# Router logits with stationary weights, one piece behind the normalization, and an earlier load of the router weights

## The reference, cut to what matters

```python
x = x + g1 * mix_lat
h = rms_norm(x, norm2_g) * (1 + sc2) + sh2        # (2048, 1024) on a core
logits = (h @ router_w).astype(float32)           # router_w: (1024, 8)
top_val, top_idx = lax.top_k(logits, 2)
top_w = softmax(top_val)
out = sum over e of comb[:, e] * swiglu(h, w1[e], w3[e], w2[e])
```

## Time and profile before

| | us |
|---|---|
| median of the 3 runs shown | 4913.67 |
| lowest, highest of them | 4563.16, 5036.57 |
| profiled execution, its time | 4566.67 |
| its span on the slowest core (core 7) | 4565.6 |
| spans of the 8 cores | 4525.7 to 4565.6 |
| TensorE busy | 3878.8 (85%) |
| DVE busy, ACT busy, GpSimd busy | 1505.7, 1522.5, 523.0 |

### The profile page before, as it was taken

The page is one execution under the profiler, slowest core; times in us unless marked ns, Lnnn a source line. Parts: engine busy times, 40 slices in busy tenths (PEclk is TensorE's granted clock), DMA queues, the critical chain, the costliest instruction groups (busy, mean ns, idle before and its releaser), DMA issues.

```text
span 4565.6 us, 77498 instructions; the slowest of 8 cores (4525.7 to 4565.6 us)
## 1 busy us (share of the span) xinstructions
PE 3878.8 (85%) x28584; PEld 2519.2 (55%) x28584; DVE 1505.7 (33%) x2750; ACT 1522.5 (33%) x2399; POOL 523.0 (11%) x634
## 2 busy tenths in 40 slices
PE   4788889657999979888695376999999999999994
PEld 2345545433444434554344255777777778787773
DVE  3634452673223264334127232111111111111114
ACT  4678822554010277884126231111111111111110
POOL 0210000540000012000007212000000000000003
PEclk8999999868999999998896567999999999999997
DMA  9586653648884526999947507999999999999997
GB/s 240 86 111 107 107 93 65 93 65 120 120 113 81 97 44 91 110 109 109 118 65 98 74 1 264 312 310 318 308 320 306 320 307 321 304 320 310 312 309 248
DMA packets 112689, 822.84 MB, mean 180 GB/s; under 512 B 14496, under 2 KB 14768, under 8 KB 41408
## 3 DMA queue, kind: packets, MB, share of 16 engines
q0 software_dynamic: 31392, 280.83, 40.2%
q1 hardware_dynamic: 80928, 537.05, 35.0%
HBM read 1016.79 MB, written 217.06 MB: 270 GB/s over the span
## 4 chain that ended last, share of the span: by engine, by line
PE 73%; ACT 7%; issue 6%; DVE 6%; DMA 4%; POOL 2%; another core or an unknown queue 2%; DVEq 0%; ACTq 0%; POOLq 0%; SPq 0%
PE psall L273 65%; PE psall L270 5%; ACT attr L298 4%; PE psall L277 2%; DMA adaw<-ada_w 2%; DMA xstage<-x 1%; DVE ntmp L301 1%; DVE attr L334 1%; ACT hT L298 1%; DVE attr L301 1%; POOL wslot L301 1%; DMA attr<-ada_w 1%; POOL sigt L301 1%; ACT wslot L298 1%
## 5 line engine op out<-in xcount | busy, mean ns | idle before, releaser
L273 PE MATMUL psall<-hs,mslot 128*128 128x256 bf16 x10304 | 1130.6, 273 | 0.5 <-ACT hs L332 0.5
L273 PEld LDWEIGHTS psall<-hs,mslot 128*128 128x128 bf16 x10304 | 1009.2, 98 | 123.0 <-issue 0.7
L298 ACT ACTIVATE sig<-psall 128x512 bf16<-128x512 f32 x322 | 192.2, 597 | 1444.7 <-PE psall L273 1444.7
L298 ACT ACTIVATE attr<-psall 128x1024 bf16<-128x1024 f32 (+1 forms) x660 | 592.1, 979 | 183.0 <-PE psall L273 180.4
L273 PE MATMUL psall<-mslot,ysp 128*128 128x512 bf16 x2576 | 559.7, 379 | 0.0
L301 DVE TENSOR_TENSOR ysp<-sig,psall 128x512 bf16<-128x512 bf16 x322 | 221.3, 687 | 866.4 <-PE psall L273 844.0
L270 PE MATMUL psall<-vaug,attr 128*128 128x129 bf16 x4640 | 393.1, 228 | 61.8 <-issue 29.3
L273 PEld LDWEIGHTS psall<-mslot,ysp 128*128 128x128 bf16 x2576 | 251.2, 98 | 298.5
L270 PEld LDWEIGHTS psall<-vaug,attr 128*128 128x128 bf16 x4640 | 278.0, 100 | 209.0 <-issue 207.4
L273 PE MATMUL psall<-hT,fslot 128*128 128x512 bf16 (+1 forms) x1760 | 352.0, 363 | 0.9 <-ACT ftf L298 0.9
L273 PE MATMUL psall<-hT,wslot 128*128 128x512 bf16 (+1 forms) x1248 | 282.6, 373 | 41.4 <-DMA wslot<-w_in 36.0
(11 more groups left out here) (190 smaller groups left out, 3611.3 us busy)
## 6 DMA issues: line engine op xcount, KB each, us to landing
mslot<-mwb SPq DMA_DIRECT2D x483, 1024.0 KB, 6.8
mwb<-mw POOLq DMA_DIRECT2D x168, 1024.0 KB, 14.9
adaw<-ada_w POOLq DMA_DIRECT2D x32, 512.0 KB, 14.9
wslot<-w_in POOLq DMA_DIRECT2D x14, 1024.0 KB, 15.6
fslot<-f POOLq DMA_DIRECT2D x7, 2048.0 KB, 17.2
xslots<-cf SPq DMA_DIRECT2D x1, 11776.0 KB, 40.6
xst<-xslots POOLq DMA_DIRECT2D x23, 512.0 KB, 11.9
oslots<-otok POOLq DMA_DIRECT2D x23, 512.0 KB, 8.3
```

The costliest lines, as they stand in the source:

```text
L273: self.P.add("pe", lambda e: e.matmul(out.ap, lhsT.ap, rhs.ap, start=start, stop=stop), reads=[lhsT, rhs], writes=[out])
L298: self.P.add("act", lambda e: e.activation(out.ap, in_.ap, func, **kw), reads=rd, writes=wr)
```

## The change

The router weights and `iota` are loaded by the SP queue instead of GpSimd's, at the start of the second layer's scan, behind a fence at which SP waits for the other engines; their place in SBUF is moved to one that is free from there on. The product is turned round: the weights, 128 x 8, are stationary and 512 normalized rows stream, one `mm` for a chunk instead of four, with the logits as [8, 512]. It is issued one piece later, so that chunk c - 1 is multiplied behind the normalization of chunk c, and `nhf` has three buffers. After chunk 7 DVE copies [8, 512] from PSUM to `lgT`, and after the last tile 16 f32 transposes of 8 x 128 bring the logits back to rows of tokens.

```diff
-    P.fence(("act", "dve", "pool"))
+    P.fence(("act", "dve", "pool", "sp") if last else ("act", "dve", "pool"))
+    if last:
+        self.wr = self.at("wr", [128, 8, 8], F32, OW + 15360)
+        self.iota_t = self.at("iota", [128, 32], F32, OW + 15616)
+        iota_d = self.din("iota", [128, 32])
+        self.dma("sp", self.iota_t.v(0), DV(iota_d[:, :], [Buf("d")]))
+        self.dma("sp", self.wr.v(0), DV(self.router_d[l // 2, :, :].rearrange("(k p) e -> p k e", p=128), [Buf("d")]))
...
-    wr = self.at("wr", [128, 8, 8], F32, OW + 8192)
-    iota_t = self.at("iota", [128, 32], F32, OW + 8448)
-    nhf = self.at("nhf", [128, 2, 512], F32, OR + 11264)
-    self.dma("pool", iota_t.v(0), DV(iota_d[:, :], [Buf("d")]))
-    self.dma("pool", wr.v(0), DV(router_d[l // 2, :, :].rearrange("(k p) e -> p k e", p=128), [Buf("d")]))
+    wr, iota_t = self.wr, self.iota_t
+    nhf = self.at("nhf", [128, 3, 512], F32, OR + 11264)
+    lgT = self.at("lgT", [128, 2048], F32, OK)
...
+        def rmm(c):
+            self.mm(V(pR.t[0:8, :], pR.v(0).bs), wr.v(0, ALL, c, ALL), nhf.v(c % 3, ALL, c % 3, ALL),
+                    start=(c == 0), stop=(c == 7))
+
         for c in range(8):
-            hv = nhf.v(c % 2, ALL, c % 2, ALL)
+            hv = nhf.v(c % 3, ALL, c % 3, ALL)
             self.norm_ap(ti, c, 1, ABv, modv, 3, out=hv)
             self.copy(h2f.v(c, ALL, c, ALL), hv, eng="pool")
-            for bi in range(4):
-                col = (ti * 4 + bi) * 8
-                self.mm(pR.v(0, ALL, S(col, col + 8)), nhf.v(c % 2, ALL, c % 2, S(bi * 128, (bi + 1) * 128)),
-                        wr.v(0, ALL, c, ALL), start=(ti == 0 and c == 0 and bi == 0), stop=(c == 7), skip=True)
+            if c >= 1:
+                rmm(c - 1)
             yield
+        rmm(7)
+        self.copy(V(lgT.t[0:8, ti * 512:(ti + 1) * 512], lgT.v(ti).bs), V(pR.t[0:8, :], pR.v(0).bs))
...
+            idv = V(self.ident_f.ap[0:8, 0:8], self.ident_f.bs)
+            for b in range(16):
+                self.tr(pR.v(0, ALL, S(b * 8, b * 8 + 8)), V(lgT.t[0:8, b * 128:(b + 1) * 128], lgT.v(b // 4).bs), idv)
             self.copy(flat(lg), pR.v(0, ALL, S(0, 128)))
```

More of the change, by code:

```diff
@@ L391, in build @@
         f2_d = [self.din(f"f2_{g}", [128, min(8, D_FF // 128 - g * 8) * D]) for g in range(3)]
-        router_d = self.din("router_w", [1, D, NEXP])
+        router_d = self.router_d = self.din("router_w", [1, D, NEXP])
         self.mw_d = [self.din(f"mw_{b}", [NEXP, 128, 4096]) for b in range(21)]
@@ L1537, in _moe_sparse @@
     self.precast(len(self.pc_list))
-    iota_d = self.din("iota", [128, 32])
     keep = OC + 16384
```

## The result

The changed kernel takes 0.9862 of the time of the one before, with a 95% interval of 0.982 to 0.9904; five more rounds gave 0.9856 (0.9819 to 0.9893). The profiled execution took 4505.1 us against 4566.7, 61.6 less. Beside this stand the medians of all executions: 4739.51 us before and 4575.58 after, of four each. Two of the four after (4646.06 and 4973.97) and two of the four before (4913.67 and 5036.57) were slow ones, in which the cores of one die or of both show a lower granted clock, and the ratios leave these out.

The account below looks back on a forecast made before the run. PE's wait on the late router weights and half-clock router pieces were taken to bound the stage. Core 0's 4563.2 us less 33.1 (load) and 33.3 (29.4 + 4.9 + 1.0 - 2.0), plus 1.1, gave 4497.9; range 4472 to 4538.

Parts of the forecast that it names:

- so I forecast no shift of it: Whole kernel: the median of three runs, 4913.67 us, lies 347 us above the profiled execution, unexplained, and was forecast not to shift.
- The load: Router weights ahead of the scan: PE's wait on their DMA goes, 33.1 us on core 0 and 44.3 on core 7.
- behind eight weight casts: Router weight load before the change: 32 KB take 56.7 us to landing, behind eight casts of 1024 KB, 42.1 us each.
- The product: Router product on PE: a piece costs 1.70 us turned against 1.75 before at the half clock, 0.85 at the full.
- rival (d): Router product costs one cycle a column, at the full clock: 6.7 us less, 4491.2 us; chance 0.10.
- rival (b): Wide f32 stream costs twice, 3.4 us a piece at the half clock: 4581.2 us, slower than before; chance 0.04.
- The clock: Router pieces no longer pull PE's clock down: three tiles gain 32.4 us, 29.4 after 1 us off for each tile.
- Rival (a): PE's clock stays half in the router pieces: the stage gains 4.5 us besides the load, 4526.7 us; chance 0.20.
- The pipelining: Router steps m = 3 to m = 6, one piece later: 25.5 us become 15.6, 9.9 gained a tile at full clock.
- without a microsecond off: The forecast's own bound for the stage at the full clock throughout: 36.9 us, 4494.3 us with core 0 slowest.
- The last tile and the end: Last router pieces gain 4.9 us, transposes to h2tok 1.0; the 16 transposes of lgT cost 2.0.
- Nothing in it has its own earlier bound: Scatter, xst load and experts behind the stage start earlier by whatever the stage saves, a microsecond for a microsecond.

Follow-up runs that it names:

- The second series: The changed kernel run once more, unchanged, against the kernel before; ratio 0.9856 (0.9819 to 0.9893), median of six executions 4509.55 us.
- both pairs of kernels: Router load by GpSimd behind the casts against SP's ahead of the scan: old product, stage 175.6 against 144.7 us; new product, 143.0 against 111.6.
- the late load: The changed kernel, but with both loads issued by GpSimd again, behind its last casts; stage 139.0 to 145.0 us, median 143.0.
- the expert weights later: The changed kernel, but SP waits for the f32 transposes of xT before the first six expert weight loads; stage 111.8 us, tail 76.7 to 87.5.

## Why the prediction was right, and where it was not

**The time.** 4498 us was forecast on the scale of the profiled execution, 0.985 of it; measured were 4505.1, and 0.9862 and 0.9856 as ratios. The median of the four executions, 4575.58, lies outside the range of 4472 to 4538. The step that failed is the one in the sum that set the median of the runs aside ("so I forecast no shift of it") and drew the range on the scale of the profiled execution alone. In its place the runs showed a median that went from 4739.51 to 4575.58, by 163.9 us, of which the kernel's part is some 62: the four executions before lie between 4563.16 and 5036.57, the four after between 4497.41 and 4973.97, and the medians fall in the gaps of these. The second series has its median at 4509.55, in the range.

That 4505.1 came within 7.2 us of the forecast is in part luck. The forecast named core 0 as the slowest, with a span of 4496.8; core 0 took 4491.4, and its stage won 63.5 us (175.3 to 111.8) where 33.1 + 33.3 = 66.4 were forecast. The slowest was core 6, for a reason that the forecast did not have (below).

**The load.** Right in kind, a little large. The wait is gone, `nhf` is awaited 2.61 us in its place. Forecast were 33.1 us on core 0; both pairs of kernels give 31 in the median, and 31.1 (old product) and 33.2 (new) on core 0. The forecast took 56.7 us as the upper bound for the early load, which was wrong: it took 13.8 to 14.8 us on four cores and 43.2 to 70.0 on the other four, where casts are in flight at that place too (nine issued between 2385 and 2470 us on core 6). It cost nothing, as a lead of 160 us covers it:

```profile
L371 SPq DMA_DIRECT2D wr<-router_w x1: 1802/1802/1802, 2393.6 to 2393.6; - x1
...
DMA to landing us min/median/max: 68.8/68.8/68.8
```

Why it was late was told in half: "behind eight weight casts" was meant as a matter of GpSimd's queue. On SP's queue at the same place it is as late, while `iota` on that queue is not.

**The product.** 1.75 against 1.70 us at one clock, so no gain from fewer records: right. Records are 0.85 us apart at the half clock and 0.43 at the full one, forecast 0.85 for two. The lower price of one cycle a column, rival (d), is out, and so is the double one, rival (b). Rival (d) was also priced wrongly: by the forecast's own schedule two pieces of 0.43 instead of 0.85 us behind each of three waits save 2.5 us a tile, not 1.7, and (d) comes to 4488.8 instead of 4491.2.

**The clock.** Right, and behind the load the largest term. Windows over the old product's router pieces have a clock of 0.50 to 0.56 with or without the stall and with or without the lag. The new one has 1.00 in tile 1; the windows of 20 us with tiles 0 and 2 have 0.83 and 0.91, and the forecast had taken 1 us off a tile for such stretches. Rival (a) is out.

**The pipelining.** 15.6 us forecast from m = 3 to m = 6, 15.9 measured in tile 1. The forecast priced turning and lag together, and never apart. The lag is worth 10.1 us with the old product and 7.5 with the new one; the turning is worth 25.6 us without the lag (144.7 - 119.1) and 23.0 with it. The two overlap by 2.6 us: together they are worth 33.1, against 33.3 forecast for all but the load. Two sums of the forecast do not come out of its own terms. At the half clock its schedule ends at 22.5 us and not 23.0, which makes rival (a) 4525.2 instead of 4526.7; and the bound at the full clock "without a microsecond off" is 32.4 + 7.0 + 1.0 - 2.0 = 38.4 us, not 36.9. Neither changes the range.

**The last tile and the end.** 9.6 us up to the end of the last record, for 8.9. The 16 small transposes take 1.15 us together, not 1.9 to 3.5; the copy to `lg` follows the last `h2tok` transposes by 1.2 us instead of 0.7. I had priced them by 128-column records; the term was 2.0 and the later copy makes it 0.5. The whole stage: forecast about 112 us on core 7, measured 111.1.

**The slowest core.** "Nothing in it has its own earlier bound", and so core 0 would be the slowest: this missed 7 of 69 us. The tail is not the same on all cores, 70.7 to 87.6 us, and the execution's slowest core is the one that has a late start of the stage (`w_out` from 2541.5 us on, against 2502.7 on the earliest) and a long tail together. Had core 6 kept the 74.7 us of the execution before, it would have ended at 4491, and core 3 with its 4495 would be the slowest. The step that failed here is "nothing in it has its own earlier bound": what the stage won, the tail gave back in part. That this is chance between executions fits the second execution of the changed kernel, with tails of 70.2 to 80.5 us against 70.4 to 81.1 before. But tails over 81.1 us were seen only in kernels with the new product (87.6, 87.3 with the late load, 87.5 with the expert weights later), so that the change has no part in them is not shown.

## What to carry to other kernels

A product with few output columns kept TensorE loading weights here; try the small operand as the stationary one, even where the time of a piece at one clock is the same, if the stretch runs at the half clock. Behind or along with a burst of large transfers a load of many short runs was late on both queues: issue it ahead of the burst, which is an edit of two lines, and ask of another queue only what its own landing time shows. When a program's time is that of its slowest core, read a saving on the core that will be the slowest afterwards, and expect its untouched stretches to differ between cores by more than the terms that you argue about.

## What the runs showed of the hardware that was not expected

A load of 1024 runs of 32 bytes by SP, issued with the first of GpSimd's eight casts, was held up as much as one by GpSimd behind them (48.4 to 59.0 us to landing against 39.8 to 45.2 in the kernel with the late load, eight cores each), although the two are different queues; `iota`, issued 0.38 us ahead of it on the same queue, took 1.6 to 3.1. TensorE busy for 24 of 27 us, mostly with weight loads and matmuls of 8 columns, has a granted clock of 0.56; with 512 columns streaming it had 1.00 in a stretch of 20 us with TensorE busy for 15.8. An f32 transpose of 8 x 128 costs 0.07 us in a row of 16. On cores of one die mostly, the stretch with the scatter has stops of TensorE of 10 to 13 us, and copies by ScalarE and VectorE that start up to 26.0 and 28.3 us late, for no work that the profile names; neither later weight loads nor another place for the transposes took them away.
